# A hybrid attention, RWKV-7 and gated-delta trunk: panel buffers that alternate between groups, gate matrices made on ScalarE, and square sums without a wait after each

## The reference, cut to what matters

```python
def gated_deltanet(p, conv_w, a_log, dt_bias, norm_w):      # p = x @ od_w_in
    qkv, z, b, a = split_cols(p, [GDN_CONV_CH, GDN_VAL_WIDTH, GDN_V_HEADS, GDN_V_HEADS])
    qkv = jax.nn.silu(causal_dwconv(qkv, conv_w))            # four taps
    q, k, v = split_cols(qkv, [GDN_KEY_WIDTH, GDN_KEY_WIDTH, GDN_VAL_WIDTH])
    ...                                                      # l2 norm of q, k
    g = -jnp.exp(a_log) * jax.nn.softplus(a + dt_bias)
    o = gated_delta_rule_chunked(q, k, v, g, beta)           # decay = exp(gc_t - gc_s), gc = cumsum(g)
    o = o * lax.rsqrt(jnp.mean(o * o, axis=-1, keepdims=True) + GDN_NORM_EPS) * norm_w
    o = o * jax.nn.silu(to_heads(z, GDN_HEAD_DIM))
    return o.reshape(bsz, t_len, GDN_VAL_WIDTH)              # then @ od_w_out, residual, layer norm
```

## Time and profile before

| | |
|---|---|
| Median of 3 runs | 3143.51 us (3138.36 to 3145.25) |
| The profiled execution: its time | 3143.37 us |
| its span in the trace | 3141.7 us |
| PE busy | 2992.0 us (95%) |
| DVE busy | 1819.8 us (58%) |
| ACT busy | 1421.3 us (45%) |
| Share of PE in the chain that ended last | 79% |

### The profile page before, as it was taken

One profiled execution on the slowest core, in us unless ns is written; L12 is line 12 of the kernel. 1 busy time (PEld: TensorE's weight loads), 2 busy tenths in 40 slices (PEclk: granted clock), 3 DMA queues, 4 the chain that ended last, 5 costly groups with the idle time before them and its releaser, 6 DMA issues.

```text
span 3141.7 us, 57226 instructions
## 1 busy us (share of the span) xinstructions
PE 2992.0 (95%) x22276; PEld 2617.4 (83%) x22276; DVE 1819.8 (58%) x2422; ACT 1421.3 (45%) x2121; POOL 13.1 (0%) x28
## 2 busy tenths in 40 slices
PE   8899998989999999999999999999998999999997
PEld 8777877778888888889898887899877888888886
DVE  4555555475455555565666666566567645555555
ACT  4443344334343444434555655455554434444442
POOL 0000000000000000000000000000000000000000
PEclk9999999999999999999999999999999999999999
DMA  6333333455555555544333334443335555555553
GB/s 227 99 100 101 98 100 121 148 201 194 188 188 189 195 193 192 191 159 140 112 127 127 123 121 141 160 149 122 111 126 186 197 194 188 191 188 190 189 188 113
DMA packets 156997, 492.08 MB, mean 157 GB/s; under 512 B 15584, under 2 KB 50528, under 8 KB 155776
## 3 DMA queue, kind: packets, MB, share of 16 engines
q1 hardware_dynamic: 154032, 476.18, 45.0%
q0 software_dynamic: 2224, 11.89, 1.0%
q10 hardware_dynamic: 544, 1.05, 0.1%
HBM read 486.96 MB, written 2.10 MB: 156 GB/s over the span
## 4 chain that ended last, share of the span: by engine, by line
PE 79%; DVE 10%; ACT 5%; issue 4%; DVEq 0%; DMA 0%; ACTq 0%; SPq 0%
PE pp L415 35%; PE mp L415 11%; PE pp L399 8%; PE mp L399 8%; PE pp L401 4%; PE mp L401 4%; DVE wl L1313 2%; DVE ws L1663 2%; ACT wh L870 1%; PE mp L798 1%; PE mp L762 1%; PE mp L746 1%; PE mp L738 1%; PE mp L804 1%; ACT ws L1131 0%
## 5 line engine op out<-in xcount | busy, mean ns | idle before, releaser
L1313 DVE TENSOR_TENSOR wl<-raw,wh 128x1024 fp32r<-128x1024 f32 (+1 forms) x936 | 1102.1, 1185 | 912.3 <-ACT wh L870 907.4
L870 ACT CAST wh<-raw 128x1024 fp32r<-128x1024 f32 (+1 forms) x936 | 944.3, 1019 | 878.4 <-PE pp L415 308.1
L415 PE MATMUL pp<-aT,wh 128*128 128x256 f32 x4704 | 906.0, 293 | 37.7 <-DVE wl L1313 21.2
L415 PEld LDWEIGHTS pp<-aT,wh 128*128 128x128 f32 x4704 | 738.8, 193 | 59.2 <-DVE wl L1313 23.4
L415 PE MATMUL pp<-aT,wl 128*128 128x256 f32 x2352 | 668.7, 284 | 0.0
L415 PEld LDWEIGHTS pp<-aT,wl 128*128 128x128 f32 x2352 | 454.0, 193 | 0.0
L415 PE MATMUL pp<-wh,hTh 128*128 128x512 f32 x896 | 360.9, 403 | 17.2 <-DVE hTl L1693 7.8
L399 PE MATMUL pp<-aT,wh 128*128 128x512 f32 x1024 | 363.0, 399 | 0.2 <-issue 0.2
L399 PE MATMUL mp<-aT,wh 128*128 128x512 f32 x1024 | 359.1, 396 | 0.0
L415 PE MATMUL pp<-wh,hTl 128*128 128x512 f32 x896 | 351.5, 392 | 0.0
L415 PE MATMUL pp<-wl,hTh 128*128 128x512 f32 x896 | 351.0, 392 | 0.0
(11 more groups left out here) (298 smaller groups left out, 2662.2 us busy)
## 6 DMA issues: line engine op xcount, KB each, us to landing
raw<-in_w_dram SPq DMA_DIRECT2D x800, 512.0 KB, 3.3
raw<-in_w_dram SPq DMA_DIRECT2D x136, 384.0 KB, 3.5
ws<-in_ln_dram POOLq DMA_DIRECT2D x8, 1024.0 KB, 7.5
out_dram<-xres SPq DMA_DIRECT2D x8, 256.0 KB, 2.0
ws<-in_lora_dram POOLq DMA_DIRECT2D x8, 192.0 KB, 2.6
xres<-in_x_dram ACTq DMA_DIRECT2D x2, 512.0 KB, 6.0
xres<-in_x_dram SPq DMA_DIRECT2D x2, 512.0 KB, 6.7
ws<-in_c_dram POOLq DMA_DIRECT2D x1, 768.0 KB, 7.4
```

Of the source, the lines that this page charges most:

```text
L415: last = mm(o, lhs, rhs, start=opens and m == 0, stop=end and kk == 1 and m == 2, skip_group_check=True)
L870: nc.scalar.copy(wh[:, q % RING, :, 0:width], raw[:, q, :, 0:width]).then_inc(S("hi_ready"), 1)
L1313: tt(wl[:, q % RING, :, 0:width], raw[:, q, :, 0:width], f(wh[:, q % RING, :, 0:width]), ALU.subtract).then_inc(S("lo_ready"), 1)
```

## The change

Four edits:

- The panels of group n use `(par, 1 - par, par)`, with `par` alternating from group to group, and the first panel of a group now needs only the panel before the last to be read out (`lag` 2, the default, in place of 1). The two loops over groups are laid out again, since a body must hold an even number of groups: groups 1 to 4 are two passes over a body of two groups, groups 6 and 7 stand in straight line. The second half of the output projection uses `pp` in the order 0, 1, 0, 1.
- `UTg` is made by ACT at visit 4 (after the sigmoid of q and k) and no more by DVE at visit 0.
- The four squares of `mean_square` write to four different 128 x 128 blocks of scratch and are followed by one wait, where each was followed by a wait for itself.
- DVE's `o_scale(1)` stands one visit later: behind the `yield`, directly ahead of `out_low(1)`.

```diff
@@ TensorE
-            def group1(n, b):
-                return blocks(n, b, "B", A, (0, 1, 0), WIDE, lag=1)
+            def group1(n, b, par):
+                return blocks(n, b, "B", A, (par, 1 - par, par), WIDE)
...
-            with pe.Fori(1, 5) as i:
-                drive(group1(i * 3 + P_L1, i * 3 + B_L1), 3 * UNITS, 0, mix1(i - 1), HOPS1)
+            with pe.Fori(0, 2) as i:
+                drive(group1(i * 6 + (P_L1 + 3), i * 6 + (B_L1 + 3), 1), 3 * UNITS, 0, mix1(i * 2), HOPS1)
+                drive(group1(i * 6 + (P_L1 + 6), i * 6 + (B_L1 + 6), 0), 3 * UNITS, 0, mix1(i * 2 + 1), HOPS1)
@@ ScalarE, mean_square
                     for h in range(4):
-                        go(sqj, os[c][:, h, :], ACT.Square, accum_out=oss[:, h:h + 1]).then_inc(S("oss"), 1)
-                        act.wait_ge(S("oss"), 8 * g + (4 * c + h + 1))
+                        st(go(XTc[:, h, :, :].rearrange("p f c -> p (f c)"), os[c][:, h, :], ACT.Square, accum_out=oss[:, h:h + 1]))
+                    st.settle()
@@ ScalarE, mix1, after the sigmoid of q and k
                 sigmoid(E1[:, 0:4, :], "qk")
                 yield
+                for c in range(TT):
+                    for h in range(4):
+                        last = go(UTg[:, c, h, :], UT, ACT.Copy, scale=head(gv, c, h))
+                        if c * 4 + h < 7:
+                            st(last)
+                last.then_inc(S("utg"), 1)
                 yield
                 yield
@@ ScalarE, group1
-                    nc.scalar.copy(zs, r2(pp[0][:, :], a=4)).then_inc(S("evacuated"), 1)
+                    nc.scalar.copy(zs, r2(pp[par][:, :], a=4)).then_inc(S("evacuated"), 1)
@@ VectorE, mix1, start
-                for c in range(TT):
-                    for h in range(4):
-                        last = ts(UTg[:, c, h, :], UT, head(gv, c, h), None, ALU.mult)
-                        if c * 4 + h < 7:
-                            st(last)
-                last.then_inc(S("utg"), 1)
                 yield
@@ VectorE, mix1, end
                 last.then_inc(S("o_sum"), 1)
+                yield
                 o_scale(1)
-                yield
                 out_low(1)
                 yield
```

More of the change, by code:

```diff
@@ L305, in trunk @@
         nw = lay(1)
-        sqj = lay(P)
         block = ctx.enter_context(nc.Block())
@@ L838, in mix1 @@
                 yield
-            def group1(n, b):
-                return blocks(n, b, "B", A, (0, 1, 0), WIDE, lag=1)
-            drive(group1(P_L1, B_L1), 3 * UNITS, 0, then(new_x(2), gates()), HOPS_GATES)
-            with pe.Fori(1, 5) as i:
-                drive(group1(i * 3 + P_L1, i * 3 + B_L1), 3 * UNITS, 0, mix1(i - 1), HOPS1)
+            def group1(n, b, par):
+                return blocks(n, b, "B", A, (par, 1 - par, par), WIDE)
+            drive(group1(P_L1, B_L1, 0), 3 * UNITS, 0, then(new_x(2), gates()), HOPS_GATES)
+            with pe.Fori(0, 2) as i:
+                drive(group1(i * 6 + (P_L1 + 3), i * 6 + (B_L1 + 3), 1), 3 * UNITS, 0, mix1(i * 2), HOPS1)
+                drive(group1(i * 6 + (P_L1 + 6), i * 6 + (B_L1 + 6), 0), 3 * UNITS, 0, mix1(i * 2 + 1), HOPS1)
             pe.wait_ge(S("mix1_out"), 8)
             drive(blocks(P_OUT1A, B_OUT1A, "A", H, (1, 0, 1, 0), WIDE), 4 * UNITS, 0, mix1(4), HOPS1)
-            drive(group1(P_L1B, B_L1B), 3 * UNITS)
-            with pe.Fori(6, 8) as i:
-                drive(group1(i * 3 + (P_L1B - 15), i * 3 + (B_L1B - 15)), 3 * UNITS, 0, mix1(i - 1), HOPS1)
+            drive(group1(P_L1B, B_L1B, 1), 3 * UNITS)
+            drive(group1(P_L1B + 3, B_L1B + 3, 0), 3 * UNITS, 0, mix1(5), HOPS1)
+            drive(group1(P_L1B + 6, B_L1B + 6, 1), 3 * UNITS, 0, mix1(6), HOPS1)
             pe.wait_ge(S("mix1_out"), 14)
-            drive(blocks(P_OUT1B, B_OUT1B, "A", H, (1, 0, 1, 0), WIDE, per=6), 24, 0, mix1(7), HOPS1)
+            drive(blocks(P_OUT1B, B_OUT1B, "A", H, (0, 1, 0, 1), WIDE, per=6), 24, 0, mix1(7), HOPS1)
             pe.wait_ge(S("mix1_out"), 16)
-            drive(blocks(P_OUT1B, B_OUT1B + 4, "A", H, (1, 0, 1, 0), WIDE, per=2, u0=24, k0=12), 8, 24)
+            drive(blocks(P_OUT1B, B_OUT1B + 4, "A", H, (0, 1, 0, 1), WIDE, per=2, u0=24, k0=12), 8, 24)
             mlp(P_MLP1, B_MLP1, 3)
@@ L1257, in mix1, with group1 @@
                 yield
-            def group1(n, before=None):
+            def group1(n, par, before=None):
                 def hook(j, after):
@@ L1266, in hook @@
                         act.wait_ge(S("conv"), before * 2)
-                    nc.scalar.copy(cbuf[:, 4 * j:4 * j + 4, 3:T + 3], r2(pp[j][:, :], a=4)).then_inc(S("evacuated"), 1)
+                    nc.scalar.copy(cbuf[:, 4 * j:4 * j + 4, 3:T + 3], r2(pp[(par + j) % 2][:, :], a=4)).then_inc(S("evacuated"), 1)
                 def z_out():
                     used(n, 3 * UNITS - 1)
-                    nc.scalar.copy(zs, r2(pp[0][:, :], a=4)).then_inc(S("evacuated"), 1)
+                    nc.scalar.copy(zs, r2(pp[par][:, :], a=4)).then_inc(S("evacuated"), 1)
                 return 3 * UNITS, wide(n), (7, 15, 23), hook, True, True, z_out
-            PER1 = 43
-            interleave(then(new_x(2), gates()), HOPS_GATES, *group1(P_L1))
+            PER1 = 58
+            interleave(then(new_x(2), gates()), HOPS_GATES, *group1(P_L1, 0))
             st.leave_straight()
[L1277 to L1280, removed]
+            with act.Fori(0, 2) as i:
+                st.enter(i, 2 * PER1)
+                interleave(mix1(i * 2, i * 2), HOPS1, *group1(i * 6 + (P_L1 + 3), 1, i * 2 + 1))
+                interleave(mix1(i * 2 + 1, i * 2 + 1), HOPS1, *group1(i * 6 + (P_L1 + 6), 0, i * 2 + 2))
+            st.leave(2)
             st.enter(0, PER1)
@@ L1283, in _ @@
             st.leave(1)
[L1284 to L1288, removed]
+            interleave(None, (), *group1(P_L1B, 1))
+            st.enter(0, 2 * PER1)
+            interleave(mix1(5, 1), HOPS1, *group1(P_L1B + 3, 0, 6))
+            interleave(mix1(6, 2), HOPS1, *group1(P_L1B + 6, 1, 7))
+            st.leave(1)
             st.enter(0, PER1)
@@ L1830, in group1 @@
                 return 3 * UNITS, wide(n), (), nothing, True, True
-            PER1 = 59
+            PER1 = 52
             interleave(then(new_x(2), gates()), HOPS_GATES, *group1(P_L1))
             st.leave_straight()
[L1835 to L1838, removed]
+            with dve.Fori(0, 2) as i:
+                st.enter(i, 2 * PER1)
+                interleave(mix1(i * 2, i * 6 + B_L1, i * 2), HOPS1, *group1(i * 6 + (P_L1 + 3)))
+                interleave(mix1(i * 2 + 1, i * 6 + (B_L1 + 3), i * 2 + 1), HOPS1, *group1(i * 6 + (P_L1 + 6)))
+            st.leave(2)
             interleave(mix1(4, B_L1 + 12, 0), HOPS1, 4 * UNITS, wide(P_OUT1A),
@@ L1842, in _ @@
             interleave(None, (), *group1(P_L1B))
[L1843 to L1846, removed]
+            st.enter(0, 2 * PER1)
+            interleave(mix1(5, B_L1B, 1), HOPS1, *group1(P_L1B + 3))
+            interleave(mix1(6, B_L1B + 3, 2), HOPS1, *group1(P_L1B + 6))
+            st.leave(1)
             interleave(mix1(7, B_L1B + 6, 3), HOPS1, 24, wide(P_OUT1B),
-                       *out_hook(P_OUT1B, B_OUT1B, (1, 0, 1, 0), 6, 0, False, False), True, begun=True)
+                       *out_hook(P_OUT1B, B_OUT1B, (0, 1, 0, 1), 6, 0, False, False), True, begun=True)
             dve.sem_inc(S("ws_free"), 1)
-            interleave(None, (), 8, wide(P_OUT1B), *out_hook(P_OUT1B, B_OUT1B + 4, (1, 0, 1, 0), 2, 24, False, True), True, begun=True, u0=24)
+            interleave(None, (), 8, wide(P_OUT1B), *out_hook(P_OUT1B, B_OUT1B + 4, (0, 1, 0, 1), 2, 24, False, True), True, begun=True, u0=24)
             layer_norm(2)
```

## The result

The changed kernel takes 3154.91 us (median of 12 runs) against 3144.29 us for the kernel before (12 runs). The ratio is 1.0031, with a 95% interval from 1.0023 to 1.0039: slower by about 10 us, where 5.3 was forecast. One run of the changed kernel (3678.61 us, granted clock 0.75) was disturbed; it is one of the 12 of the median and is not in the ratio.

The account below looks back on a forecast made before the run. It took the chain over DVE and ACT to the first transposes as the bound between groups, not PE's z-copy wait. Boundaries 2.5, output projection 3.25, group 5 -1.1, clock +0.6 gave +5.3 on 3143.37: 3148.7 us, range 3139 to 3156.

Parts of the forecast that it names:

- chain behind the late scaling: Later z copy and taps: 4 x 0.6 = 2.5 at mixed-group boundaries, plus 1.1 and 1.15 at tails into the output projection.
- gate matrices on ScalarE: At visit 4, eight products at 0.26 us each, hidden before DVE wants the third copy: nothing; upper bound 5.6 us.
- clock on the last half unit: Ahead of the z copy, a lowered clock costs 0 to 1.3 us in each of 4 places; 0.35 each taken, 1.4.
- the jump back: In the group loops, half as many jumps, DVE's idle 0.59 covered by its wait for ACT: nothing.
- output projection, group 5's start: After the second low-part wait taps bound, +1.0; at group 5 the residual wait goes, net about -1.1, and clock -0.8.
- The mechanism: At each tail, PE's gap of 3.1 us moves ahead of the last half unit; z copy 1.15 later, taps 0.6.
- The rival of the wait: At the panels, PE's waits were the cost: 13.7 and 2.9 us go, 16.6 gained, 3127 us; chance 0.06.
- the bound of 1.3: Ahead of the z copy, the most a lowered clock on the last half unit can cost per place, in us.
- The bound of +0.5: In the group loops, the most the new layout costs per boundary in us, since longer code has to be fetched.

Follow-up runs that it names:

- filled kernel: The changed kernel with 28 needless transposes of the identity on TensorE ahead of its wait for the scaled second chunk: 3151.35 us, ratio 1.0016.
- straight kernel: The changed kernel with groups 1 to 4 written out in straight line in place of two passes over a two-group body: 3152.57 us, ratio 1.0021.
- straight code: The kernel before with groups 1 to 4 written out in straight line in place of its loop: 3141.72 us, ratio 0.9981.
- version with the gate matrices at visit 3: The changed kernel with the scaling at its old visit and the gate matrices on DVE at visit 3, loops kept: 3139.94 us, ratio 0.9987.
- best version: The changed kernel with scaling at its old visit, gate matrices on DVE at visit 3 and groups 1 to 4 in straight line: 3130.96 us, ratio 0.9957.

## Why the prediction was right or wrong

Forecast and measured terms. The chain is the filled kernel's six ordinary intervals against before (+5.6 with its jump's interval set at its neighbours' 104.73), less ScalarE's share; the clock is the sum of what the six spans above exceed 2.12 by.

```
                                        forecast   profiled
chain behind the late scaling             +4.75      +3.65
gate matrices on ScalarE                   0         +1.97
clock on the last half unit               +1.4       +4.55
the jump back (and what is left over)      0         +2.48
output projection, group 5's start        -0.9       -4.04
after the last z copy                      0         -0.18
```

The sums are +5.3 and +8.4. (The forecast's 3.25 for the output projection is split here: the two tails that lead into it stand in the chain.)

**The mechanism was right.** "The gap has moved from one side of the last half unit to the other": 3.01 us measured, 3.1 forecast; scaling behind two splits; taps 3.74 us behind the z copy, 3.7 forecast; from the first transposes to the next z copy 78.9 us in the filled kernel (104.73 - 25.84) against 77.7 before, +1.2, forecast +1.15. Reading what stands behind a waiting instruction on each engine gave the chain in the loop to 0.1 us: without clock and ScalarE's share its intervals grew by 0.64 to 0.66, forecast 0.6 (the first, which has no tail ahead of it, by 1.18). The term as a whole came out 1.1 too high, since those of groups 6 and 7 grew by 0.37 and 0.15 only. The change also writes these two groups out, which the forecast gave no worth, and they are 0.35 under the groups in the loop in the changed and the filled kernel; no run writes them out by themselves. The experiments confirm it from both sides: the moved line alone costs 18 us on the kernel before, and taking it out of the changed kernel gives 14.

**The rival of the wait.** Free panel buffers gave 3 us of 16.6. They work at group 5's start; at the boundaries PE waits for a split instead, ahead of the first transposes. (Its premise was off as well: the z copy's gap is not PE's largest, a wait of 4.7 us for `xres` stands in the same window.)

**Clock: right mechanism, wrong size.** The step was "between 0 and 1.3 us in each of 4 places. I take 0.35 each". It was 0.44, 0, 0.90, 0.78, 1.27 and 1.16, and in six places, since the tails before the output projection count as well. The straight kernel shows 1.45 to 1.55 in five places, over the bound of 1.3. I had the earlier trace rows and five of eight such gaps with a clock under 1 (seven of the eight were 2.68 us or more, the eighth 2.40, and not all 2.7); taking those at their price, 5/8 of the 1.3 in six places, would have given 4.9.

**Loops: the step failed.** "DVE's idle 0.59 ahead of its gate matrices at a jump is now covered by its wait for ACT. Nothing". I looked at VectorE only. The interval with the jump is 2.2 us longer than its share of chain and clock (107.87 - 104.74 - 0.90), and in it ScalarE's jump holds the chain for 2.8 us. Half as many jumps are no saving when one costs nearly what the four intervals of before gained from straight code (2.4 us in all, of which the jumps are half). The bound of +0.5 came from VectorE's row.
The Trainium skill (Runtime: NRT & Kernel Launch, Instruction fetch mechanics) says that a taken branch to a target outside the pages held at the moment must fetch it first. That fits what was seen, a doubled body and an engine that idles with its target far away, but no run here varies the length of the body by itself.

**Gate matrices: the step failed by its own bookkeeping.** "DVE wants that copy at 1794.03, shifted by 0.6 to 1794.6": I shifted the demand and left the supply. But the copies come behind sigmoids that wait for VectorE's taps, so both shift alike and the cover was 0.6 less. ScalarE's list is held 2.36 us (1804.66 - 1802.30), 0.295 each and not 0.26, and VectorE waits 0.30 to 0.39 us in each group. The +1.97 is the sum of six of these waits; that they lengthen the kernel by as much is argued from the trace, for the run that takes the products off ScalarE again can't be told from the changed kernel.
The Trainium skill (VectorE: DVE Perf Modes, on the TRN2 errata) gave the estimate of 0.29 each; the trace agrees with it better than with the squares, which I had followed.

**Group 5's start** gained more than forecast: the residual wait of 2.9 us is gone, and the waits for the low part with it. How the remaining 4 us split between that and the clock stays open; kernels with the old buffers show 190.1 to 193.0 there, those with the new ones 187.8 to 190.1.

## What to carry to other kernels

A wait that an engine is seen in may be only the place where a late chain becomes visible: before removing it, ask what the same engine will wait for next, and follow the chain to the instruction that is really late. Don't put work of the chain behind bulk work in an ordered list to save a short idle time; put the bulk work, like the gate matrices here, into an idle stretch of the engine instead. Read the cost of a jump back on every engine, not on one, and shift supply and demand together when a chain moves.

## What the runs showed of the hardware that was not expected

- A jump back over a body of two groups held ScalarE for 2.79 us in the chain and made the interval 2.2 us longer (3.6 to 3.7 in the version with the gate matrices at visit 3); over a body of one, VectorE's added 0.4 us to a gap of 0.21. Writing the loops out gave 2.3 us (changed), 4.6 (before) and 9.0 (the best version) in the medians.
- The same wait of VectorE for ScalarE's high part was 0.90 to 0.96 us in the loops of the kernel before and 0.68 or 0.69 in its straight code.
- A gap of 3.0 us of TensorE ahead of work on the path was followed by a granted clock of 0.50 to 0.81 in five of six places, which are stretches partly (the one of 0.50 wholly) at 1.2 GHz, and cost 0.4 to 1.3 us each beyond the gap, up to 1.55 in the straight kernel. Work that nobody reads in the gap brought the 1.00 back in all six places and 3.6 us in the median.
